# A decoder layer with 32 experts: gate-up of expert 31 moved ahead of down of expert 30, and a place of its own for the last down weights

## What is computed

```python
logits = (xt @ router_w + router_b)
top_logit, top_e = lax.top_k(logits, 4)          # 4 of 32 experts for each token
top_w = jax.nn.softmax(top_logit, axis=-1)
...
gu = xb @ w_gu[e] + b_gu[e]                      # 1024 -> 2048, for each of the 32 experts
gate = jnp.minimum(gu[:, :1024], 7.0)
up = jnp.clip(gu[:, 1024:], -7.0, 7.0)
act = gate * jax.nn.sigmoid(1.702 * gate) * (up + 1.0)
y = act @ w_dn[e] + b_dn[e]                      # 1024 -> 1024
out = out.at[tok].add(y * w[:, None])            # weighted sum over a token's experts
...
x = layer_norm(DEEPNORM_ALPHA * x + ffn, ln2_g, ln2_b)
```

## Time and profile before

| | us |
|---|---|
| median of three runs | 1132.6 |
| lowest and highest run | 1130.32 and 1132.66 |
| span of the profiled execution | 1131.7 |
| TensorE (PE) busy | 1062.0 (94%) |
| VectorE (DVE) busy | 239.4 (21%) |
| ScalarE (ACT) busy | 151.1 (13%) |
| DMA, mean rate over the span | 377 GB/s |

### The profile page before, as it was taken

The page is one execution under the profiler, slowest core; times in us unless marked ns, Lnnn a source line. Parts: engine busy times, 40 slices in busy tenths (PEclk is TensorE's granted clock), DMA queues, the critical chain, the costliest instruction groups (busy, mean ns, idle before and its releaser), DMA issues.

```text
span 1131.7 us, 14828 instructions
## 1 busy us (share of the span) xinstructions
PE 1062.0 (94%) x5442; PEld 463.3 (41%) x5443; DVE 239.4 (21%) x734; ACT 151.1 (13%) x316; POOL 20.5 (2%) x49
## 2 busy tenths in 40 slices
PE   7999999989999999999999989999999999999895
PEld 6777644333534333333232323434333334343331
DVE  3354663201111111110111101111111111111014
ACT  2043611010101010100010100101010101010020
POOL 2000210000000000000000000000000000000000
PEclk9999999989999999999999989999999999999999
DMA  9723459969999999999999999999999999999993
GB/s 312 268 112 76 189 203 385 403 271 396 426 425 426 426 426 426 426 426 426 426 426 424 427 395 428 427 426 427 429 426 426 426 422 426 426 425 426 426 427 131
DMA packets 49412, 426.45 MB, mean 377 GB/s; under 512 B 5114, under 2 KB 9003, under 8 KB 16587
## 3 DMA queue, kind: packets, MB, share of 16 engines
q1 hardware_dynamic: 48666, 425.37, 90.9%
q10 hardware_dynamic: 720, 0.74, 0.2%
HBM read 425.04 MB, written 1.05 MB: 376 GB/s over the span
## 4 chain that ended last, share of the span: by engine, by line
PE 63%; DMA 33%; DVE 2%; issue 1%; ACT 1%; SPq 0%; DVEq 0%
PE PB L789 60%; DMA WB<-in_w_down_dram 29%; DMA WB<-in_w_gate_up_dram 3%; PE PB L1164 1%; DMA X<-in_x_dram 0%; PE PB L796 0%; DVE S L1569 0%; PE PB L893 0%; DVE S L1825 0%; DVE S L1603 0%; DVE K L1816 0%; DVE X L1608 0%; PE PB L894 0%; PE PB L895 0%; DVE K L1586 0%
## 5 line engine op out<-in xcount | busy, mean ns | idle before, releaser
L789 PE MATMUL PB<-WB,S 128*64 128x512 f32 (+5 forms) x3456 | 757.5, 593 | 40.0 <-DMA WB<-in_w_down_dram 30.9
L789 PEld LDWEIGHTS PB<-WB,S 128*64 128x64 f32 (+2 forms) x3456 | 258.7, 139 | 517.4 <-issue 438.7
L1702 DVE TENSOR_SCALAR S<-PB 128x512 f32<-128x512 f32 (+1 forms) x34 | 23.5, 691 | 482.8 <-PE PB L789 482.8
L789 PE MATMUL PB<-S 32*64 32x512 f32 (+5 forms) x456 | 104.5, 588 | 1.5 <-ACT S L710 1.4
L714 ACT ACTIVATE S<-S 128x512 f32<-128x512 f32 x32 | 20.2, 630 | 471.8 <-DVE S L1702 471.8
L1744 DVE COPY S<-PB 64x512 f32<-64x512 f32 x31 | 21.2, 684 | 281.0 <-PE PB L789 281.0
L789 PEld LDWEIGHTS PB<-S,X 128*128 128x128 f32 x512 | 59.7, 192 | 12.6 <-issue 12.2
L789 PE MATMUL PB<-S,X 128*128 128x128 f32 x512 | 63.9, 278 | 0.1
L789 PE MATMUL PB<-S,WB 128*128 128x256 f32 (+2 forms) x336 | 60.1, 377 | 0.4 <-ACT S L548 0.4
L789 PEld LDWEIGHTS PB<-S 32*64 32x64 f32 (+5 forms) x456 | 30.9, 147 | 62.9 <-issue 58.8
L730 ACT ACTIVATE S<-PB 64x512 f32<-64x512 f32 x31 | 18.4, 593 | 249.1 <-PE PB L789 249.1
(11 more groups left out here) (214 smaller groups left out, 332.5 us busy)
## 6 DMA issues: line engine op xcount, KB each, us to landing
WB<-in_w_gate_up_dram SPq DMA_DIRECT2D x128, 2048.0 KB, 25.8
WB<-in_w_down_dram SPq DMA_DIRECT2D x128, 1024.0 KB, 21.9
WB<-in_w_in_dram SPq DMA_DIRECT2D x3, 2048.0 KB, 15.3
WB<-in_w_in_dram SPq DMA_DIRECT2D x1, 2144.0 KB, 10.3
WB<-in_w_in_dram SPq DMA_DIRECT2D x2, 1024.0 KB, 10.6
WB<-in_w_out_dram SPq DMA_DIRECT2D x2, 1024.0 KB, 10.3
WB<-in_w_out_dram SPq DMA_DIRECT2D x1, 2048.0 KB, 7.9
WB<-in_w_in_dram SPq DMA_DIRECT2D x1, 1040.0 KB, 12.2
```

The costliest lines, as they stand in the source:

```text
L789: return mm_(o, l, r, start=start, stop=stop, skip_group_check=True)
L1702: ts(g, gate, LIMIT, None, ALU.min).then_inc(s[g_ok], 1)
```

## The change

Expert 31's gate-up is loaded and computed before expert 30's down. The last four loads of weights become gate-up 30, gate-up 31, down 30, down 31. Down 31 goes to `dn_last`, the second half of `reg_a`, where the gate-up chunks 2 and 3 of expert 30 lay; its first two chunks wait for the use of chunk 2 there, the other two for chunk 3. The activations of expert 31 go to `actT_last`, and its down result to PB4 instead of PB7, so that both can stand beside those of expert 30. The loops of TensorE, ScalarE and VectorE run 14 times, and a last pass (experts 29 and 30), without down 30, is written out behind them.

```diff
+        actT_last = take(512, c=4, s=P)
+        dn_last = reg_a[:, GU // 2:].rearrange("p (k n) -> p k n", k=KT)
...
-            with sp.Fori(PAIRS - 1 - IN_ORDER, PAIRS - 1) as i:
+            with sp.Fori(PAIRS - 1 - IN_ORDER, PAIRS - 2) as i:
...
+            count_extra_blocks(N_EXPERTS - 3)
+            next_gu(PAIRS - 2, 1)
+            next_dn(PAIRS - 2, 1)
+
             count_extra_blocks(N_EXPERTS - 2)
-            next_dn(PAIRS - 1, 0)
-
+            kk = KT // DN_CHUNKS
+            for c in range(DN_CHUNKS):
+
+                g = 2 + c // 2
+                sp.wait_ge(s["guc"], (N_EXPERTS - 2) * GU_CHUNKS + g + 1)
+                sp.wait_ge(s["xguc"], use_by_extra_blocks(g))
+                sp.dma_start(dn_last[:, kk * c:kk * c + kk, :],
+                             dn_v[N_EXPERTS - 1][:, c // 2, 2 * (c % 2):2 * (c % 2) + 2, :]).then_inc(s_dnl[1][c], 16)
...
-            with act.Fori(0, PAIRS - 1) as i:
+            def odd_expert(i):
...
+            with act.Fori(0, PAIRS - 2) as i:
+                odd_expert(i)
+                even_expert(i)
                 expert_output(0, 2 * i + 3)
+            odd_expert(PAIRS - 2)
+            even_expert(PAIRS - 2)
...
-            act_columns(5, N_EXPERTS)
+            act_columns(5, N_EXPERTS, actT_last)
             extra_blocks(N_EXPERTS - 1)
+            expert_output(0, N_EXPERTS - 1)
...
+            with pe.Fori(0, PAIRS - 2) as i:
+                odd_expert(i)
+                even_expert(i)
                 down(0, i + 2, 2 * i + 3)
+
+            odd_expert(PAIRS - 2)
+            even_expert(PAIRS - 2)
...
+            pe.wait_ge(s["actT"], N_EXPERTS - 1)
             for c in range(GU_CHUNKS):
                 pe.wait_ge(s_gul[1][c], 16 * PAIRS)
                 gate_up_chunk(c, 1).then_inc(s["guc"], 1)
-                if c == 0:
-                    pe.wait_ge(s["ysb_ok"], N_EXPERTS)
-                    pe.wait_ge(s["ysb_dv"], N_EXPERTS - 1)
-                if c < 2:
-                    outputs_of_30(c)
                 if c == 2:
                     last_weight_transposes()
...
-            extra_blocks(1, PAIRS, N_EXPERTS - 1, "xg_ok", 2 * PAIRS, N_EXPERTS - 1)
-            down(1, PAIRS, N_EXPERTS)
+            extra_blocks(1, PAIRS, N_EXPERTS - 1, "xg_ok", 2 * PAIRS, N_EXPERTS - 2, dn_last)
+
+            pe.wait_ge(s["ysb_ok"], N_EXPERTS - 1)
+            pe.wait_ge(s["ysb_dv"], N_EXPERTS - 2)
+            for c in range(DN_CHUNKS):
+                pe.wait_ge(s_dnl[0][c], 16 * PAIRS)
+                down_chunk(c).then_inc(s["dn_used"], 1)
+
+            pe.wait_ge(s["actT"], N_EXPERTS)
+            for c in range(DN_CHUNKS):
+                pe.wait_ge(s_dnl[1][c], 16 * PAIRS)
+                down_chunk(c, PB[4], actT_last, dn_last).then_inc(s["dn_used"], 1)
+                if c == 0:
+                    pe.wait_ge(s["ysb_ok"], N_EXPERTS)
+                    pe.wait_ge(s["ysb_dv"], N_EXPERTS - 1)
+                if c < 2:
+                    outputs_of_30(c)
```

More of the change, by code:

```diff
@@ L435, in _ @@
                     next_gu(i, par)
-            count_extra_blocks(N_EXPERTS - 2)
-            next_dn(PAIRS - 1, 0)
+            count_extra_blocks(N_EXPERTS - 4)
+            next_dn(PAIRS - 2, 0)
+            next_gu(PAIRS - 2, 0)
+            count_extra_blocks(N_EXPERTS - 3)
+            next_gu(PAIRS - 2, 1)
+            next_dn(PAIRS - 2, 1)
+            count_extra_blocks(N_EXPERTS - 2)
+            kk = KT // DN_CHUNKS
[5 more added lines that the diff above has]
+                             dn_v[N_EXPERTS - 1][:, c // 2, 2 * (c % 2):2 * (c % 2) + 2, :]).then_inc(s_dnl[1][c], 16)
             sp.wait_ge(s["guc"], (N_EXPERTS - 1) * GU_CHUNKS)
@@ L714, in sigmoid, with act_columns @@
                 act.activation(act_sb, gt, ACT.Gelu_apprx_sigmoid).then_inc(s["sig"], 1)
-            def act_columns(bank, n):
+            def act_columns(bank, n, actT=actT):
                 act.wait_ge(s["at"], n)
@@ L757, in _, with even_expert @@
                 expert_output(1, 2 * i + 2)
+            def even_expert(i):
                 sigmoid(2 * i + 3)
@@ L772, in _ @@
             sigmoid(N_EXPERTS)
-            act_columns(5, N_EXPERTS)
+            act_columns(5, N_EXPERTS, actT_last)
             extra_blocks(N_EXPERTS - 1)
+            expert_output(0, N_EXPERTS - 1)
             act.wait_ge(s["dn_used"], N_EXPERTS * DN_CHUNKS)
-            act.activation(y_last[64:128, :], PB[7][64:128, :], ACT.Copy).then_inc(s["ysb_ok"], 1)
+            act.activation(y_last[64:128, :], PB[4][64:128, :], ACT.Copy).then_inc(s["ysb_ok"], 1)
         @block.tensor
@@ L1131, in gate_up, with down_chunk, extra_down_chunk @@
                 gate_up_bias(e).then_inc(s["gu"], 1)
-            def down_chunk(c):
+            def down_chunk(c, bank=PB[7], actT=actT, weights=dn_slot):
                 for k in range(2 * c, 2 * c + 2):
                     for h in range(2):
-                        ins = mm(PB[7][64 * h:64 * h + 64, :], actT[:, k % 4, 64 * (k // 4):64 * (k // 4) + 64],
-                                 dn_slot[:, k, 512 * h:512 * h + 512], k == 0, k == KT - 1)
+                        ins = mm(bank[64 * h:64 * h + 64, :], actT[:, k % 4, 64 * (k // 4):64 * (k // 4) + 64],
+                                 weights[:, k, 512 * h:512 * h + 512], k == 0, k == KT - 1)
                 return ins
-            def extra_down_chunk(c):
+            def extra_down_chunk(c, dn_slot):
                 for k in range(2 * c, 2 * c + 2):
@@ L1227, in extra_combine, with extra_blocks @@
                         mm(acc(b, h)[:, :], CTx[64 * h:64 * h + 64, b, :], yx[64 * h:64 * h + 64, :], False, False)
-            def extra_blocks(e, loaded, t, pb4_pb6_copied, copies, outputs_copied):
+            def extra_blocks(e, loaded, t, pb4_pb6_copied, copies, outputs_copied, weights=dn_slot):
                 count = pe.value_load(nx[0:1, t:t + 1] if isinstance(t, int) else nx[0:1, bass.ds(t, 1)], min_val=0,
@@ L1249, in extra_blocks @@
                             pe.wait_ge(s_dnl[e][c], 16 * loaded)
-                            extra_down_chunk(c).then_inc(s["xdnc"], 1)
+                            extra_down_chunk(c, weights).then_inc(s["xdnc"], 1)
                         extra_combine()
@@ L1266, in _, with odd_expert @@
             down(0, 1, 1, first=True)
-            with pe.Fori(0, PAIRS - 1) as i:
+            def odd_expert(i):
                 gate_up(1, i + 1, 2 * i + 2)
@@ L1787, in _, with pair @@
             expert_output(0, 1)
-            with dve.Fori(0, PAIRS - 1) as i:
+            def pair(i):
                 first_extra_slots(2 * i + 1)
@@ L1798, in _ @@
                 next_one_hots(i + 1)
+            with dve.Fori(0, PAIRS - 2) as i:
+                pair(i)
                 expert_output(0, 2 * i + 3)
+            pair(PAIRS - 2)
             t = N_EXPERTS - 1
@@ L1808, in _ @@
             extra_blocks(t, N_EXPERTS)
+            expert_output(0, N_EXPERTS - 1)
             dve.wait_ge(s["dn_used"], N_EXPERTS * DN_CHUNKS)
-            cp(y_last[0:64, :], PB[7][0:64, :]).then_inc(s["ysb_dv"], 1)
+            cp(y_last[0:64, :], PB[4][0:64, :]).then_inc(s["ysb_dv"], 1)
             for b in range(TB):
```

## The result

The changed kernel takes 1142.19 us (median of 4 runs, 1139.53 to 1143.59) against 1132.29 us (4 runs, 1130.32 to 1132.66): ratio 1.0083, 95% interval 1.0064 to 1.0102. The change makes the kernel 9.9 us slower. The profiled execution took 1141.26 us, with a span of 1139.2 us.

The account below looks back on a forecast made before the run. The tail was taken as bound by TensorE's own work, after a weight-stream bound up to 1069.08 us. Terms -0.7 + 0.3 + 2.9 + 1.0 + 3.4 = +6.9 on 1132.6 gave 1139.5 us, range 1131.0 to 1145.0.

Parts of the forecast that it names:

- refills behind jumps: Likeliest case: jumps over unused extra-token code at experts 29 to 31 meet late code pieces; 1136.5 to 1145 us, chance 0.50.
- copy wait of expert 31: TensorE's wait for expert 31's activations copy goes, because down 30 now stands behind the transposes: -0.7 us.
- (1): Expert 29: the jump passes over a whole code piece; 3.1 us late, DMA waits swallow all but 0.3.
- (2): Expert 30: border two instructions ahead of the jump test, jump lands in the following piece at once: +2.9 us.
- (3): Expert 31: jump lands near a piece's end, down 30 crosses a border after six matmuls; pause 2.3 replaces 1.3: +1.0 us.
- clock: TensorE's granted clock drops after long stalls, costing 1.7 us each; two drops taken: +3.4 us.
- The price of a miss: Time from the transposes' start before a jump until TensorE resumes, if the code piece is missing: 4.55 us taken.
- the pause of before: TensorE's 1.30 us pause without releaser, seven matmuls into down 31, taken as waiting for its last code piece.
- A: Rival: refills are hidden, the copy wait (0.7) goes and the 1.3 us stall leaves the tail: 1130.6 us; chance 0.22.
- B: Rival: a miss costs 3.2 us from when the code is reached; +3.4, 1136.0 us; chance 0.20.
- C: Rival: all prices at the upper bound, 6.7 us a miss and a third clock drop: 1147.6 us; chance 0.08 with beyond.
- The load order: The same 16 weight chunks in another order, gate-up 31's last chunk arriving just in time: costed at nothing.

Follow-up runs that it names:

- moved by 140: Changed kernel with 35 one-column filler matmuls (140 TensorE instructions) between the loop's end and the written-out pass: 1132.15 us, ratio 0.9991 to before.
- moved by 28: Changed kernel with 7 filler matmul calls (28 TensorE instructions) between the loop's end and the written-out pass: 1141.0 us, one run.
- Moved by 44: Kernel before with 11 filler matmuls (44 TensorE instructions) behind its loop, ahead of gate-up 31, order unchanged: 1135.16 us, ratio 1.0031 to before.

## Why the prediction was right, and where its terms were off

The forecast was 1139.5 us with a range of 1131.0 to 1145.0; measured were 1142.19. The case that it called likeliest, refills behind jumps, is what happens: the places ahead of down 29 and of gate-up 31, six pieces after 1040 us (it said five), a clock below 1.0 behind each, and no wait for weights after 1075 us. Written-out code in the old order reproduces it, moved code in the new order removes it. The mechanism was right and its sizes were off. Of its +6.9 us against the measured +9.9, term by term:

| term | predicted | measured |
|---|---|---|
| copy wait of expert 31 | −0.7 | −0.69 |
| (1) expert 29, less the swallowed DMA waits | +0.3 | +1.75 |
| (2) expert 30 | +2.9 | +5.22 |
| (3) down 30's border for down 31's | +1.0 | −0.98 |
| clock | +3.4 | +4.67 |

The error in (3) has the other sign than the rest and hides 2.0 us of them. With (3) as forecast the measured time would have been 1144.2 us, so the range held with less room than 1142.19 suggests.

**The price of a miss** was mis-sized in (1) and (2). I took 4.55 us from the transposes to the first matmul behind the jump; it measured 6.72 (1044.50 to 1051.22) and 6.86 (1077.84 to 1084.70). The row I took it from was in the same place of the program, as I argued, but not in the same position to a border: there the jump stayed inside the pieces at hand and ran into the border seven matmuls later. Nor was it "under the same DMA load". In before the last weights landed at 1110.6 us, and the fetch began 2.2 us behind the end of the branch (1110.07 behind 1107.86); with weights still streaming it begins 3.7 and 3.9 us behind the start of the branch. That is most of the 2.2 us that each miss cost more. The upper bound of 6.7, drawn from the piece at 282 us, was the right value; I had set it aside. At expert 29 the DMA waits swallowed 2.84 us as worked out, and 0.67 more went with them, since one group of 96 matmuls takes 20.82 us, and the four groups of before take 21.47 together (10.52 and three times 3.65).

**Term (3) has the wrong sign.** I put the border six matmuls into down 30. The trace shows only a slow spot, about 13 matmuls in: 31 matmuls in 7.61 us where 32 take 7.09, and 0.95 us more than in the run moved by 140 up to the first addition (1106.72 to 1116.41, 9.69 us, against 1099.00 to 1107.74, 8.74 us). The piece was fetched at 1107.9 and came nearly in time. In exchange the pause of before left the tail, which is worth 1.93 and not 1.3 us.

**The clock** fell twice, as predicted, but it cost 2.17 and 2.50 us and not 1.7 each. Each time it was at half for 6.8 us, against 3.4 us behind the early pauses that I took the price from. Of the 6.8 us the part in the stall costs nothing; 4.4 and 5.1 us fell on matmuls, and about half of that is the loss. The length of the stall alone does not tell it: moved by 28, the stall of 3.27 us came with 6.8 us at half clock and that of 4.95 us with 3.4.

**The rivals.** A (hidden refills, 1130.6) is what the order does once the code lies well: 1132.15 and 1131.01 us, within 0.2% of before. Of the 2.0 us that it adds, the part of the pause is seen where the pause is taken out of the old order (1129.81 us); the part of the copy wait is seen in no median. B's price (3.2 us a miss) is excluded by both stalls; its premise, that a piece is asked for only once it is reached, is the one that fits the traces. C (all at the upper bound, 1147.6) had the right price for a miss but three drops of the clock and a loss at (3). The load order was costed at nothing, and that held for gate-up 31 and both downs, which no run with the new loads and the early issue waits for; gate-up 30's last chunk started 0.1 to 1.2 us later in the four kernels without stalls or fillers at the start, which takes back a part or all of the 0.7 us.

**What stays open.** Counting bytes gives the borders only to within some 15 instructions: before's pause and the slow spot in down 30 call for offsets that differ by 14. The branches of 4.2 us instead of 6.2 seem to have two causes. Moved by 44, the weights end at 1107.3 us, and the fetch begins 1.7 us behind the branch's start, much as behind the landings of other kernels in the last 4 us of their weights (1.8 to 2.2 us). Moved by 28, the weights run on to 1112.7 us, and the 1.8 us fit a piece asked for a little ahead of the branch; no run tests that. The scatter of gate-up 30's last chunk has no cause either.

## What to carry to other kernels

This kernel, whose TensorE program of before is 17.3 pieces and its loop about 4.4, pays for straight code by where its jumps lie. Before a loop pass is written out, count its instructions, and look in the trace for the instruction queue's pieces and for waits on "issue" behind a taken branch; a jump should start and land far from a border, in neighbouring pieces, or the jumped-over code should stand elsewhere. Test an idea about order with the code held in place, or a gain of 0.7 us is looked for through a shift that costs ten. Here the runs without stalls show the copy wait gone and no gain in time.

## What the runs showed of the hardware

- A jump to a piece that is not there costs more than the fetch. In the changed kernel the fetch starts 3.7 and 3.9 us after the branch begins (1048.43 behind 1044.77, 1082.07 behind 1078.18), takes 1.0 to 1.1 us, and TensorE goes on 1.8 and 1.6 us after it ended. In the two cases of 4.2 us it starts 1.7 to 1.8 us after the branch begins and the rest is the same.
- The next piece seems to be asked for only when a piece is entered. At all 18 jumps over extra-slot code that led into a new piece at the experts 29 to 31 while weights streamed, the fetch of the piece behind the landing starts 3.2 to 3.6 us behind the end of the branch, whether the branch was short or long. In the last 4 us of the weights it is 1.8 to 2.2 us (four jumps), and after them 0.7 us (moved by 44, and before with the written-out pass). A landing right before a border stalls for nearly as long as a miss (4.95 us), although the branch takes 318 ns.
- One pass of the loop is about as long as what the change writes out, 1,124 instructions or 4.4 pieces (an estimate from that count), and no piece is fetched between 340 us and the end of the loop: the loop keeps running on what TensorE holds.
- The placement of code is worth more than the edit here: the four kernels that kept the order of before, and differ from it in fillers, in a written-out pass or in one unused block of code, range from 1129.81 to 1140.92 us.
